# A change to an attention kernel: the weights of rows 4 to 7 are transposed in 32x32 blocks on VectorE and regrouped through DRAM

## The chip, the cores and the metric

The kernel runs on one core of one Trainium2 chip. The metric is the time of one execution on the device in microseconds, the median of repeated runs. The core has TensorE (PE in the profile: matrix products; PEld is its loading of stationary operands), VectorE (DVE), ScalarE (ACT), GpSimd (POOL) and SyncE (SP, which here only issues transfers). They run side by side and wait for one another on semaphores. Operands lie in SBUF (called `arena` here), products are written to PSUM (`psum`, eight banks of 512 float32 columns by 128 partitions). Sixteen DMA engines move data between SBUF and DRAM.

## What is computed

The reference is one inference step of two layers: a gated linear recurrence, and behind it a "forgetting attention" layer over 1024 new positions and, for eight decoding sequences, over 1024 cached positions each. The change concerns the attention over the new positions alone. Cut to that part:

```python
def forgetting_attention(q, k_all, v_all, c_all):
    def one_block(args):                       # 128 query positions
        qi, start = args
        s = jnp.einsum('bqhd,bkhd->bhqk', qi, k_all) * scale
        mask = key_pos[None, :] <= q_pos[:, None]
        logits = jnp.where(mask, s + (c_q[..., :, None] - c_t[..., None, :]), -jnp.inf)
        p = jax.nn.softmax(logits, axis=-1)
        return jnp.einsum('bhqk,bkhd->bqhd', p, v_all)
    out = lax.map(one_block, (qb, starts))
```

There are 16 heads of 64 channels, and everything is float32. The product with the values sums over key positions, so the weights `p`, which come out with query positions on the partitions, must be turned so that key positions lie on the partitions.

## The kernel before

The attention is done in eight pairs of heads (`p` = 0 to 7). Within a pair there are eight rows: row `i` holds the 128 query positions of block `i` against the `i + 1` key blocks up to it, for both heads `x`. Rows are worked as follows, each step on its own engine:

- `scores(p, i)` (L2333, PE) writes the logits to PSUM. Rows 0 to 3 alternate between two halves of banks 2 to 5; rows 4 to 7 fill all four banks, so that such a row can't begin before the one ahead has left them.
- `row_max(p, i)` (L1694 to L1705, DVE) adds the forget bias and the causal mask and takes the maximum.
- `soft(p, i)` (L1175 to L1184, ACT) takes the exponential, sums, and scales the weights; they go to `weights` in SBUF.
- `turn_rows(p, i)` (L2340, PE) transposes them, one 128x128 product with the identity for each head and key block, into the row's banks.
- `turn_a` (L1190, ACT, head 0) and `turn_v` (L1713, DVE, head 1) copy the transposed weights to `pt` in SBUF.
- `weighted(p, m)` (L2356, PE) multiplies rows `2m` and `2m + 1` together with the values, and `fin` (L1724, L1726, DVE) takes the result.

Between these steps, TensorE has other work in hand that fills the time in which a row passes through DVE and ACT: the projections of the next pair, in units of eight products (`kq`, `vg`; L2028, 28 units in a pair, each with an add or copy behind it, L1358 on DVE or L934 on ACT), the means of squares for the norms (L2295), the decoding part (`decode`, L2389), and in the last pair the output projection (`y_part`, L2535). The decoding part streams cached keys and values: SP loads key pages into a ring of two slots (`k_in`, L582, 512 KB each), GpSimd multiplies them with the query (`times_q`, L857), DVE reduces them (`score`, L1767), which frees the slot; value pages come in fours (`v_in`, L588, 4 x 512 KB). SP also loads the projection weights of the pairs ahead (`load_wb`, L471), DVE scales them (`scale_w`, L468), and GpSimd forms sums of them (`block_sums`, L721 to L724) that a unit needs.

The order on every engine is written out by hand in the functions `pair` of the engines; no scheduler changes it. Each engine works its own list in order, and an instruction that waits holds up all that stands behind it on that engine. SP's list of transfers is such a list too.

## Time and profile before

| | |
|---|---|
| median of 3 runs | 1558.84 us (1558.44 to 1559.26) |
| the profiled execution's own time | 1557.86 us |
| its span | 1556.1 us |
| granted TensorE clock, mean over the span | 0.998 |
| TensorE busy | 1525.4 us, 98% |
| VectorE busy | 995.0 us, 64% |
| ScalarE busy | 713.6 us, 46% |
| GpSimd busy | 429.5 us, 28% |
| DMA | 242.32 MB, mean 156 GB/s |

The profile is of one execution; times inside it are counted from the start of its span. The recurrence layer and the first projections take about the first 756 us; the eight pairs follow, about 89 us each, and the rest of the output projection ends the program. Busy time alone doesn't say what a change is worth: the chain of work that ended last and the idle time ahead of each group do that. Matrix products overlap each other, so the mean duration of one in a group is longer than the distance from one to the next; the distance is read from the timeline.

### The profile page before, as it was taken

Reading aid. Unit: us, or ns where it says so; the run is one execution under the profiler, and the core shown is the slowest. Engines: PE = TensorE matmul, PEld = TensorE weight load, DVE = VectorE, ACT = ScalarE, POOL = GpSimd, SP = SyncE. Lnnn points to the kernel's source line nnn. Section 1 sums busy time; section 2 is a strip of 40 time slices with the busy share of each in tenths; the row PEclk is TensorE's granted clock in tenths of the full one; section 3 lists DMA queues with packets and bytes.
Section 4 is the critical chain, followed back from the end, with each engine's and each line's share of the span. In section 5 each row is a group of like instructions: output and inputs, shape, how many; then the busy total and the mean of one; then the engine's idle time right before and its main releaser. Section 6 shows DMA issues by size and latency. Waiting matters only on the chain.

```text
span 1556.1 us, 23869 instructions
## 1 busy us (share of the span) xinstructions
PE 1525.4 (98%) x8769; PEld 1137.0 (73%) x8769; DVE 995.0 (64%) x1947; ACT 713.6 (46%) x1412; POOL 429.5 (28%) x335
## 2 busy tenths in 40 slices
PE   7999999999999999999999999999999999998998
PEld 6888888888888865447777777777777777774443
DVE  6869687876868673226375766667686776765321
ACT  4445554454555542221455655555455564555100
POOL 5022212121231001012253425343343334422200
PEclk9999999999999999999999999999999999999999
DMA  9692936658293743323333445464444546366231
GB/s 270 177 265 78 271 115 199 175 152 242 74 296 102 226 163 99 89 63 100 102 99 111 137 164 176 136 203 136 160 131 134 173 147 193 150 214 231 84 136 56
DMA packets 254085, 242.32 MB, mean 156 GB/s; under 512 B 23162, under 2 KB 219962, under 8 KB 253970
## 3 DMA queue, kind: packets, MB, share of 16 engines
q1 hardware_dynamic: 242834, 204.21, 43.0%
q0 software_dynamic: 11136, 36.59, 6.7%
q8 instruction: 70, 1.15, 0.3%
q14 instruction: 45, 0.37, 0.1%
HBM read 212.63 MB, written 95.24 MB: 198 GB/s over the span
## 4 chain that ended last, share of the span: by engine, by line
PE 90%; DVE 5%; ACT 2%; issue 2%; DMA 0%; SPq 0%; POOL 0%; DVEq 0%; ACTq 0%; POOLq 0%
PE psum L2028 46%; PE psum L2052 7%; PE psum L2535 7%; PE psum L2333 5%; PE psum L2356 4%; PE psum L2340 4%; PE psum L2105 3%; PE psum L2295 2%; PE psum L2389 2%; PE psum L1991 2%; PE psum L2175 1%; PE psum L2116 1%; PE psum L2191 1%; PE psum L2203 1%; ACT arena L1175 1%
## 5 line engine op out<-in xcount | busy, mean ns | idle before, releaser
L2028 PE MATMUL psum<-arena 128*128 128x252 f32 (+1 forms) x3472 | 812.2, 384 | 0.7 <-DVE arena L1358 0.6
L2028 PEld LDWEIGHTS psum<-arena 128*128 128x128 f32 x3472 | 641.6, 190 | 121.1 <-issue 30.5
L1358 DVE TENSOR_TENSOR arena<-arena,psum 128x252 f32<-128x252 f32 (+1 forms) x310 | 130.7, 422 | 216.8 <-PE psum L2028 208.0
L857 POOL TENSOR_TENSOR arena<-arena 128x1024 f32<-128x1024 f32 x64 | 160.4, 2506 | 225.0 <-DMA arena<-k_pages 198.1
L1175 ACT ACTIVATE arena<-psum,arena 128x256 f32<-128x256 f32 (+7 forms) x128 | 93.8, 739 | 122.0 <-DVE arena L1705 121.7
L934 ACT COPY arena<-psum 128x252 f32<-128x252 f32 (+1 forms) x124 | 45.9, 371 | 169.4 <-PE psum L2028 169.4
L2535 PE MATMUL psum<-arena 128*128 128x512 f32 x256 | 114.2, 597 | 0.0
L2052 PE MATMUL psum<-arena 128*128 128x512 f32 x256 | 113.0, 594 | 0.1
L721 POOL TENSOR_TENSOR arena<-arena 128x512 f32<-128x512 f32 x31 | 39.9, 1288 | 249.7 <-issue 129.1
L1184 ACT ACTIVATE arena<-arena 128x256 f32<-128x256 f32 (+7 forms) x128 | 92.4, 769 | 2.1
L2052 PEld LDWEIGHTS psum<-arena 128*128 128x128 f32 x256 | 47.5, 190 | 57.4 <-issue 56.5
L2535 PEld LDWEIGHTS psum<-arena 128*128 128x128 f32 x256 | 46.9, 190 | 56.0 <-issue 55.5
L987 ACT ACTIVATE arena<-arena 128x1024 f32<-128x1024 f32 x48 | 50.6, 1055 | 78.0 <-DVE arena L1402 77.9
L1713 DVE COPY arena<-psum 128x128 f32<-128x128 f32 (+3 forms) x64 | 48.4, 756 | 53.2 <-PE psum L2340 53.1
L2333 PE MATMUL psum<-arena 64*128 64x512 f32 (+3 forms) x384 | 79.3, 517 | 2.1 <-DVE arena L1713 2.0
L2340 PE MATMUL psum<-arena 128*128 128x128 f32 x576 | 76.4, 276 | 4.6 <-ACT arena L1184 4.6
L2340 PEld LDWEIGHTS psum<-arena 128*128 128x128 f32 x576 | 64.9, 141 | 20.4 <-ACT arena L1184 10.9
L1767 DVE TENSOR_REDUCE arena<-arena 128x16 f32<-128x1024 f32 x64 | 77.6, 1213 | 0.0
L2356 PE MATMUL psum<-arena 128*64 128x256 f32 (+1 forms) x640 | 69.5, 362 | 1.6 <-DVE arena L1815 1.6
L2356 PEld LDWEIGHTS psum<-arena 128*64 128x64 f32 x640 | 43.1, 136 | 30.2 <-issue 10.5
L1705 DVE CUSTOM_DVE_ANT_0 psum<-psum,arena 128x128 f32<-128x128 f32 (+3 forms) x128 | 63.4, 536 | 2.2
L1190 ACT COPY arena<-psum 128x128 f32<-128x128 f32 (+3 forms) x64 | 41.3, 646 | 47.2 <-PE psum L2340 45.5
(262 smaller groups left out, 2136.0 us busy)
## 6 DMA issues: line engine op xcount, KB each, us to landing
k_pages<-in_cache_k SPq DMA_DIRECT2D x64, 512.0 KB, 6.7
v_pages<-in_cache_v SPq DMA_DIRECT2D x64, 512.0 KB, 7.2
arena<-k_pages SPq DMA_DIRECT2D x64, 512.0 KB, 3.6
arena<-v_pages SPq DMA_DIRECT2D x64, 512.0 KB, 5.8
arena<-in_w_in_a SPq DMA_DIRECT2D x32, 512.0 KB, 7.0
arena<-in_x_prompt SPq DMA_DIRECT2D x16, 512.0 KB, 7.4
arena<-in_w_kv SPq DMA_DIRECT2D x16, 512.0 KB, 5.5
arena<-in_w_in_b SPq DMA_DIRECT2D x16, 512.0 KB, 7.1
```

The source lines that it names most:

```text
L857: pool.tensor_tensor(k_ring[:, m % 2], k_ring[:, m % 2], q_all[:, m % S:m % S + 1, :].broadcast_to([P, PAGES, P]), ALU.mult).then_inc(kq_m ...
L1175: ins = act.activation(weights[:, x, 0:n], rows[:, x, 0:n], ACT.Exp, bias=top[:, at:at + 1], scale=-1.0, accum_out=total[:, at:at + 1])
L1184: act.activation(weights[:, x, 0:n], weights[:, x, 0:n], ACT.Copy, scale=inv[:, at:at + 1]).then_inc(p_set, 1)
L1358: dve.tensor_tensor(out, more, bank[n % 2][:, 0:size(u)], ALU.add).then_inc(of.by_dve, 1)
L1705: dve.tensor_tensor_reduce(out=rows[:, x, lo:n], in0=rows[:, x, lo:n], in1=c, scale=1.0, scalar=part[:, at:at + 1] if lo else -LOW, op0=AL ...
L1767: dve.tensor_reduce(lg[:, b, :, 0:PAGES].rearrange("p x j -> p j x"), k_ring[:, m % 2].rearrange("p j (x d) -> p j x d", x=2), AX.X, ALU.a ...
L2028: ins = pe.matmul(bank[n % 2][:, 0:size(u)], w[:, k, :], x[:, k, :], start=(k == 0 and r in (0, 1, 3, 4)), stop=(k == HK - 1), skip_group_ ...
L2052: ins = pe.matmul(dst[0:rows, :], o_heads[h][:, rows_of(t)], w_o[:, h, 512 * j:512 * j + 512], start=(h == 0 or lo == AH - 1), stop=(h == ...
L2333: ins = pe.matmul(dst[:, x, lo:hi], q_t[p % 2][rows, cols(i)], k_t[p % 2][rows, lo:hi], start=True, stop=True)
L2340: ins = pe.transpose(row_banks(i)[:, x, cols(j)], weights[:, x, cols(j)], ident)
L2356: ins = pe.matmul(bank[6][rows, lo:2 * P], v_cur[:, j, rows], pt[:, x, SLOT[m] + j, lo:2 * P], start=(j == 0), stop=(j == i), skip_group_c ...
L2535: ins = pe.matmul(dst, o_y[h][:, cols(t)], w_ob[h][:, 512 * j:512 * j + 512], start=(h == 0), stop=(h == AH - 1), skip_group_check=True)
```

## The change

The weights of rows 0 to 3 are still transposed by TensorE, from a smaller buffer (`low_weights`). For rows 4 to 7:

- `soft` leaves the scaled weights in the row's PSUM banks.
- `turn_blocks` (DVE) transposes them out of PSUM into `weights`, once for each head. It transposes within 32x32 blocks only: what is left is to bring each group of 32 partitions' blocks to the partitions of its key positions. `turn_a` and `turn_v` are gone for these rows.
- `store_row` (SP) writes `weights` to a scratch tensor in DRAM, `block_rows`, with four transfers, each from 32 partitions, laid out so that the blocks lie in the wanted order; `load_row` reads the row back into `pt` with one transfer of 128 partitions. A row of block `i` is 2 x (i + 1) x 128 x 128 float32: 0.66, 0.79, 0.92 and 1.05 MB for rows 4 to 7, once out and once in.
- `weighted(p, 2)` and `weighted(p, 3)` wait for the loads (`pt_moved`), and read their moving operand in runs of 32 columns.
- `scores` of rows 5 to 7 and of the next pair's row 0 wait for `blocks_turned`; `turn_blocks` of a row waits until the row ahead is stored (`rows_stored`), since `weights` is one buffer.

Around this the lists of all five engines are ordered anew. `weighted(p, 2)` moves from behind `scores(p, 6)` to behind `scores(p, 7)`; `weighted(p - 1, 3)` moves from just behind `scores(p, 0)` to behind `vg` units 11 and 12; `decode(p - 1, 0)` behind it. The scaling of the four projection weights on DVE, the sums of `w_k` and `w_q` on GpSimd, and the last two key pages of a pair on SP move too.

The core of the diff, part by part; most of the lines that only change places in the lists are left out, since the rows below show them. Layouts and SP's list:

```diff
+        def block_len(i):
+            return 2 * (i + 1) * 32
+
+        def group_len(m):
+            return block_len(2 * m) + block_len(2 * m + 1)
+
+        def moving(m, x, j):
+
+            first, both = 2 * m, j <= 2 * m
+            if m == 0:
+                at, row_step, inner = x * P, 2 * P + x * P, [[1, P]]
+                at, row_step = (at, row_step) if both else (2 * P + x * 2 * P + P, 0)
+            elif m == 1:
+                at, row_step, inner = PT_AT[1] + x * 8 * P + j * 2 * P + (0 if both else P), P, [[1, P]]
+            else:
+                row_step, inner = block_len(first) + 32 * x, [[group_len(m), 4], [1, 32]]
+                at = PT_AT[m] + x * 32 * (first + 1) + 32 * j + (0 if both else row_step)
+            return bass.AP(pt.tensor, pt.offset + at, [pt.ap[0], *([[row_step, 2]] if both else []), *inner])
...
+            def store_row(p, i):
+                sp.wait_ge(blocks_turned, 2 * high_row(p, i))
+                if p:
+                    sp.wait_ge(pt_moved, MOVES * high_row(p - 1, i))
+                n = block_len(i)
+                dst = block_rows[i - LOW_ROWS, :, 0:4 * n].rearrange("(r l) (g n) -> g l r n", r=4, g=4)
+                for g in range(4):
+                    src = weights[32 * g:32 * g + 32, 0:4 * n].rearrange("p (r n) -> p r n", r=4)
+                    sp.dma_start(dst[g], src).then_inc(rows_stored, 16)
+
+            def load_row(p, i):
+
+                m, n = i // 2, block_len(i)
+                sp.wait_ge(rows_stored, STORES * high_row(p, i))
+                if i % 2 == 0:
+                    sp.wait_ge(pv_done, 4 * p + m)
+                at = i % 2 * block_len(i - 1)
+                dst = pt[:, PT_AT[m]:PT_AT[m] + 4 * group_len(m)].rearrange("p (g n) -> p g n", g=4)[:, :, at:at + n]
+                src = block_rows[i - LOW_ROWS, :, 0:4 * n].rearrange("p (g n) -> p g n", g=4)
+                sp.dma_start(dst, src).then_inc(pt_moved, 16)
...
-                    k_in(m - 1)
+                    k_in(m - 2, m - 1)
...
+                k_in(m + 5)
+                store_row(p, 6)
+                load_row(p, 6)
+                store_row(p, 7)
+                load_row(p, 7)
```

GpSimd and ScalarE:

```diff
+                if p + 1 < PAIRS:
+                    sums_of_kq(p + 1)
+                if p:
+                    times_q(m - 2)
...
-                if p + 2 < PAIRS:
-                    sums_of_kq(p + 2)
...
+                dst = low_weights if i < LOW_ROWS else rows
...
-                    ins = act.activation(weights[:, x, 0:n], rows[:, x, 0:n], ACT.Exp, bias=top[:, at:at + 1], scale=-1.0,
+                    if 0 < i < LOW_ROWS:
+                        act.wait_ge(t_done, 2 * low_row(p, i - 1) - 1 + x)
+                    ins = act.activation(dst[:, x, 0:n], rows[:, x, 0:n], ACT.Exp, bias=top[:, at:at + 1], scale=-1.0,
...
-                    act.activation(weights[:, x, 0:n], weights[:, x, 0:n], ACT.Copy, scale=inv[:, at:at + 1]).then_inc(p_set, 1)
+                    act.activation(dst[:, x, 0:n], dst[:, x, 0:n], ACT.Copy, scale=inv[:, at:at + 1]).then_inc(p_set, 1)
...
+                act.wait_ge(t_done, 2 * low_row(p, i) - 1)
+                act.copy(low_pt(i, 0), row_banks(i)[:, 0, 0:(i + 1) * P].rearrange("p (j n) -> p j n", n=P)).then_inc(pt_a, 1)
```

VectorE:

```diff
+            def turn_blocks(p, i, *xs):
+
+                if high_row(p, i) > 1:
+                    dve.wait_ge(rows_stored, STORES * (high_row(p, i) - 1))
+                n = block_len(i)
+                for x in xs:
+                    dve.wait_ge(p_set, 2 * row(p, i) - 1 + x)
+                    out = weights[:, 0:4 * n].rearrange("p (r x j l) -> p x j r l", r=4, x=2, l=32)[:, x]
+                    dve.transpose(out, row_banks(i)[:, x, 0:(i + 1) * P].rearrange("p (j r l) -> p j r l", r=4, l=32)).then_inc(blocks_turned, 1)
...
-                dve.tensor_tensor(g_raw, g_raw, g_tmp, ALU.mult).then_inc(gate_v.sem, 1)
-                dve.wait_ge(gate_v.sem, gate_v.at("silu", p))
-                me.chain(dve.tensor_copy(g_smp[p % 2], g_raw[:, T:N]))
+                me.did(dve.tensor_tensor(g_raw[:, 0:MID], g_raw[:, 0:MID], g_tmp[:, 0:MID], ALU.mult))
+                me.did(dve.tensor_tensor(g_smp[p % 2], g_raw[:, T:N], g_tmp[:, T:N], ALU.mult))
+                dve.tensor_tensor(o_t[:, OWN + p % 2, MID:T], g_raw[:, MID:T], g_tmp[:, MID:T], ALU.mult).then_inc(gate_v.sem, 1)
...
-                turn_v(p, 7)
-                top_of(p, 0)
+                if nxt:
+                    shift(p, 0)
+                turn_blocks(p, 7, 0)
                 if nxt:
                     norm(p + 1, 1)
-                    shift(p, 0)
+                turn_blocks(p, 7, 1)
+                if not nxt:
```

TensorE:

```diff
-                before = TT * p + (i if i >= TT // 2 else max(i - 1, 0))
-                if before:
-                    pe.wait_ge(pt_a, before)
-                    pe.wait_ge(pt_v, before)
+                if 2 <= i <= LOW_ROWS:
+                    last_low = low_row(p, i - 1 if i == LOW_ROWS else i - 2)
+                    pe.wait_ge(pt_a, last_low)
+                    pe.wait_ge(pt_v, last_low)
+                elif i > LOW_ROWS or p:
+                    pe.wait_ge(blocks_turned, 2 * (high_row(p, i - 1) if i > LOW_ROWS else high_row(p - 1, TT - 1)))
...
             def weighted(p, m):
                 i = 2 * m + 1
-                pe.wait_ge(pt_a, row(p, i))
-                pe.wait_ge(pt_v, row(p, i))
+                if i < LOW_ROWS:
+                    pe.wait_ge(pt_a, low_row(p, i))
+                    pe.wait_ge(pt_v, low_row(p, i))
+                else:
+                    pe.wait_ge(pt_moved, MOVES * high_row(p, i))
...
-                        ins = pe.matmul(bank[6][rows, lo:2 * P], v_cur[:, j, rows], pt[:, x, SLOT[m] + j, lo:2 * P],
+                        ins = pe.matmul(bank[6][rows, lo:2 * P], v_cur[:, j, rows], moving(m, x, j),
...
                 if p:
+                    weighted(p - 1, 3)
+                turn_rows(p, 1)
+                if p:
+                    decode(p - 1, 0)
+                vg(p, 13)
+                if p:
                     turn_num(p - 1, 0)
...
-                turn_rows(p, 7)
+                vg_n(5)
+                weighted(p, 2)
```

TensorE's list, from the end of one pair to `weighted(p - 1, 3)` of the next. Before, from `turn_top` (L2366) and the last two units (L2028) of a pair over `scores(p, 0)` (L2333) to `weighted(p - 1, 3)` (L2356):

```order
L2366 MATMUL psum<-arena 8x128 [waits lg_set,items_taken]
L2028 MATMUL psum<-arena 128x264 [waits b_units_taken_v]
L2028 MATMUL psum<-arena 128x264 x3
L2371 MATMUL psum<-arena 128x8 [waits items_taken]
L2028 MATMUL psum<-arena 128x264 [waits b_units_taken_v]
L2028 MATMUL psum<-arena 128x264 x3
L2333 MATMUL psum<-arena 128x128 [waits pt_v,pt_a,norm_done]
L2333 MATMUL psum<-arena 128x128
L2356 MATMUL psum<-arena 64x256 [waits fin_done,pt_v,pt_a]
L2356 MATMUL psum<-arena 64x256 x13
```

After the change, the same place begins later in the pair: `scores(p, 0)`, `vg` 9, the first half of `turn_k`, `vg` 10 and `turn_rows(p, 0)` stand ahead of these rows, which show the second half of `turn_k` (L2379), `scores(p, 1)` (L2413), `turn_smp` (L2385), units 11 and 12 (L2106), and `weighted(p - 1, 3)` (L2439):

```order
L2379 MATMUL psum<-arena 128x128 [waits norm_done,items_taken]
L2379 MATMUL psum<-arena 128x128 x3
L2413 MATMUL psum<-arena 128x256 [waits blocks_turned]
L2413 MATMUL psum<-arena 128x256
L2385 MATMUL psum<-arena 8x128 [waits norm_done,items_taken]
L2386 MATMUL psum<-arena 8x128
L2106 MATMUL psum<-arena 128x264 [waits b_units_taken_a]
L2106 MATMUL psum<-arena 128x264 x3
L2106 MATMUL psum<-arena 128x264 [waits b_units_taken_v]
L2106 MATMUL psum<-arena 128x264 x3
L2439 MATMUL psum<-arena 64x256 [waits fin_done,pt_moved]
L2439 MATMUL psum<-arena 64x256 x13
```

Four projection units, `scores(p, 1)` and the small transposes now stand between `scores(p, 0)` and the product of row 7, and that product waits for the load.

SP's list at the change of pairs. Before, from the loads of `w_k` and `w_q` of one pair to the value pages in the next:

```order
L471 DMA arena<-in_w_kv 128x8x128 [waits b_units_done]
L471 DMA arena<-in_w_in_b 128x8x128
L582 DMA arena<-k_pages 128x1024 [waits k_free] x2
L594 DMA arena<-c_rows 128x1024 [waits max_done]
L591 DMA arena<-c_rows 128x1024 [waits max_done]
L582 DMA arena<-k_pages 128x1024 [waits k_free]
L588 DMA arena<-v_pages 128x1024 [waits num_done]
L588 DMA arena<-v_pages 128x1024 x3
```

After, from the key page `k_in(m + 5)` over the stores and loads of rows 6 and 7 to the value pages (L477 has the two loads ahead of it):

```order
L621 DMA arena<-k_pages 128x1024 [waits k_free]
L667 DMA block_rows<-arena 32x4x448 [waits pt_moved,blocks_turned]
L667 DMA block_rows<-arena 32x4x448 x3
L678 DMA arena<-block_rows 128x4x448 [waits pv_done,rows_stored]
L667 DMA block_rows<-arena 32x4x512 [waits pt_moved,blocks_turned]
L667 DMA block_rows<-arena 32x4x512 x3
L678 DMA arena<-block_rows 128x4x512 [waits rows_stored]
L633 DMA arena<-c_rows 128x1024 [waits max_done]
L630 DMA arena<-c_rows 128x1024 [waits max_done]
L621 DMA arena<-k_pages 128x1024 [waits k_free] x2
L627 DMA arena<-v_pages 128x1024 [waits num_done]
```

The forget biases (`c_rows`) and two key pages now stand behind the load of row 7, which waits for its four stores.

VectorE's list behind row 7's maximum. Before, from the units behind it to the scaling of `w_q` (L468), the last of the pair:

```order
L1358 TENSOR_TENSOR arena<-arena,psum 128x252 [waits b_units_done,b_units_taken_v] x2
L1767 TENSOR_REDUCE arena<-arena 128x8x2 [waits kq_mult]
L1671 SCALAR_TENSOR_TENSOR arena<-arena 128x1032 [waits rs_done]
L1358 TENSOR_TENSOR arena<-arena,psum 128x252 [waits b_units_done,b_units_taken_v]
L1713 COPY arena<-psum 128x8x128 [waits t_done]
L1782 TENSOR_REDUCE arena<-psum 8x1 [waits items_done]
L1671 SCALAR_TENSOR_TENSOR arena<-arena 128x1032 [waits rs_done]
L1788 TENSOR_TENSOR arena<-arena,psum 128x72 [waits items_done]
L1358 TENSOR_TENSOR arena<-arena,psum 128x264 [waits b_units_done,b_units_taken_a]
L1680 TENSOR_TENSOR arena<-arena 64x8 [waits items_done,norm_done]
L1680 TENSOR_TENSOR arena<-arena 64x8
L468 TENSOR_TENSOR arena<-arena 128x1024 [waits w_q_loaded]
```

After, from the unit behind it to the product for the new score (L1748), which is the last of the pair:

```order
L1426 TENSOR_TENSOR arena<-arena,psum 128x252 [waits b_units_done,b_units_taken_v]
L1802 TENSOR_TENSOR arena<-arena,psum 128x256 [waits pv_done]
L1859 TENSOR_REDUCE arena<-psum 8x1 [waits items_done]
L1739 SCALAR_TENSOR_TENSOR arena<-arena 128x1032 [waits rs_done]
L1426 TENSOR_TENSOR arena<-arena,psum 128x252 [waits b_units_done,b_units_taken_v]
L1865 TENSOR_TENSOR arena<-arena,psum 128x72 [waits items_done]
L1790 STREAM_TRANSPOSE arena<-psum 128x8x4x32 [waits p_set,rows_stored]
L1739 SCALAR_TENSOR_TENSOR arena<-arena 128x1032 [waits rs_done]
L1790 STREAM_TRANSPOSE arena<-psum 128x8x4x32 [waits p_set,rows_stored]
L1426 TENSOR_TENSOR arena<-arena,psum 128x264 [waits b_units_done,b_units_taken_a]
L1748 TENSOR_TENSOR arena<-arena 64x8 [waits items_done,norm_done]
L1748 TENSOR_TENSOR arena<-arena 64x8
```

The copy of head 1 (L1713) has become two transposes (L1790), with one of the norms (L1739) between them, and the scaling of `w_q` and one reduction (L1767) have left this place.

## Rows read from the trace of the kernel before

**Rows 1.** Profile page, part 1: busy time of each engine (TensorE is PE).

```profile
PE 1525.4 (98%) x8769; PEld 1137.0 (73%) x8769; DVE 995.0 (64%) x1947; ACT 713.6 (46%) x1412; POOL 429.5 (28%) x335
```

**Rows 2.** Profile page, part 4: the chain that ended last, by engine.

```profile
PE 90%; DVE 5%; ACT 2%; issue 2%; DMA 0%; SPq 0%; POOL 0%; DVEq 0%; ACTq 0%; POOLq 0%
```

**Rows 3.** Windows: length, busy us of each engine, granted clock, DMA share, GB/s.

```profile
1195.87:1285.22 89.35, 88.43 (x598) 67.21 (x597) 64.05 (x137) 49.29 (x105) 36.45 (x24) 1.00 0.49 154
```

**Rows 4.** Timeline, TensorE, places of that pair: start, us, line, tile, count.

```profile
1201.58 0.60 PE L2301 MATMUL psum<-arena 128*128 128x128 f32 x4
...
1238.21 1.35 PE L2340 MATMUL psum<-arena 128*128 128x128 f32 x10
1239.40 0.29 PE L2376 MATMUL psum<-arena 128*128 128x16 f32 x2
...
1263.22 2.61 PE L2356 MATMUL psum<-arena 128*64 128x256 f32 x24
...
1270.92 1.99 PE L2333 MATMUL psum<-arena 64*128 64x512 f32 x8
...
1279.20 1.91 PE L2340 MATMUL psum<-arena 128*128 128x128 f32 x16
1280.95 0.27 PE L2366 MATMUL psum<-arena 128*8 128x128 f32 x1
1281.06 1.95 PE L2028 MATMUL psum<-arena 128*128 128x264 f32 x8
...
1285.22 0.49 PE L2333 MATMUL psum<-arena 64*128 64x128 f32 x4
```

**Rows 5.** Groups by form, TensorE: count, busy us, mean ns of one.

```profile
L2340 PE MATMUL psum<-arena 128*128 128x128 f32 x576 | 76.4, 276 | 4.6 <-ACT arena L1184 4.6
...
L2105 PE MATMUL psum<-arena 128*128 128x128 f32 x448 | 59.9, 277 | 0.0
```

**Rows 6.** Groups by form, VectorE (DVE): copies of L1713, one transpose.

```profile
L1713 DVE COPY arena<-psum 128x1024 f32<-128x1024 f32 x8 | 9.8, 1226 | 6.9 <-PE psum L2340 6.9
...
L1713 DVE COPY arena<-psum 128x640 f32<-128x640 f32 x8 | 6.6, 826 | 3.3 <-PE psum L2340 3.3
...
L1299 DVE STREAM_TRANSPOSE arena<-arena 128x128 f32<-128x128 f32 x1 | 0.3, 311 | 0.0
```

**Rows 7.** Timeline, ScalarE (ACT), the softmax of row 7.

```profile
1274.72 1.12 ACT L1175 ACTIVATE arena<-psum,arena 128x1024 f32<-128x1024 f32 x1 [0.44 <-DVE arena L1705]
...
1277.53 2.19 ACT L1184 ACTIVATE arena<-arena 128x1024 f32<-128x1024 f32 x2
```

**Rows 8.** Timeline, SyncE: four loads issued in a row.

```profile
1250.64 1.93 SPq L588 DMA_DIRECT2D arena<-v_pages  x4
```

**Rows 9.** Line L588, those four loads: time from issue to landing.

```profile
DMA to landing us min/median/max: 3.7/5.3/6.7
```

**Rows 10.** Line L582, 54 loads of 512 KB: time to landing.

```profile
DMA to landing us min/median/max: 3.4/3.6/8.8
```

**Rows 11.** Line L834, eight stores of 512 KB: time to landing.

```profile
DMA to landing us min/median/max: 3.8/8.6/9.0
```

**Rows 12.** Window in which four loads stream: DMA share and GB/s.

```profile
1256.00:1258.00 2.00, 2.00 (x11) 0.99 (x8) 1.43 (x4) 1.06 (x1) 0.00 (x0) 1.00 1.03 395
```

**Rows 13.** Timeline, SyncE, the load of w_v in the same pair.

```profile
1213.72 0.38 SPq L471 DMA_DIRECT2D arena<-in_w_kv  x1
```

**Rows 14.** Timeline, TensorE: one wait and the unit behind it.

```profile
761.06 0.66 PE L2340 MATMUL psum<-arena 128*128 128x128 f32 x2 [1.79 <-ACT arena L1184]
...
762.73 3.04 PE L2028 MATMUL psum<-arena 128*128 128x264 f32 x8
```

**Rows 15.** Windows around that wait, and one in the last pair.

```profile
758.67:761.50 2.83, 1.04 (x7) 0.64 (x5) 0.80 (x5) 2.12 (x9) 0.00 (x0) 1.00 0.00 0
761.50:764.90 3.40, 3.30 (x10) 2.60 (x10) 0.29 (x1) 1.30 (x4) 0.74 (x1) 0.50 0.00 0
1431.00:1437.00 6.00, 4.40 (x24) 2.11 (x22) 5.20 (x18) 3.01 (x7) 1.12 (x1) 1.00 0.06 25
```

178 lines of the change are left out of this document (90 added, 88 removed).

## The prediction

> **What bounds the kernel now.** I read the page's busy times first, then its chain, then windows of one pair, then the timeline inside it. TensorE is busy for 98% of the span [rows 1] and makes 90% of the chain that ended last [rows 2]. In the pair that I take as the pattern, from 1195.87 to 1285.22 us, it is busy for 88.4 of 89.35 us, at a granted clock of 1.00, the 2.4 GHz level [rows 3]. DVE has 25 us to spare in the pair, ACT 40, the DMA engines half their time. So work taken from TensorE's list comes off the time one for one, as long as rows and transfers keep up with the shorter list. That is the whole question.
>
> **What leaves TensorE.** The mean of one transpose is 276 ns [rows 5], but they overlap. The timeline has the distance: the ten of row 4 begin at 1238.21 and the next group at 1239.40, which is 1.19 us; the sixteen of row 7 take 1279.20 to 1280.95, 1.75 us [rows 4]. Rows 5 and 6, with 12 and 14, lie between, so four rows take 4 x (1.19 + 1.75) / 2 = 5.88 us, in eight pairs 47.0 us. Nothing hides them. This is the gain, and no other product leaves: the 416 removed are these.
>
> The Trainium skill ("TensorE: Matmul & The Clock Gate", Part 4: PE-mode transpose) gives a transpose as about 275 ns in one kernel's context. The mean in [rows 5] is the same figure, the distance in [rows 4] is 109 to 119 ns; a sum by the page's figure would take 416 x 0.275 = 114 us off, the sum by the distance 47.
>
> **What the products with the values cost.** Rows 4 to 7 are now read in runs of 32 columns instead of 128. No product here reads such runs. The nearest are those of L2105, whose moving operand is two runs of 64: mean 277 ns against the 276 of the transposes, which read 128 in one [rows 5]. I take 0. If runs half as long doubled nothing at 64, a doubling at 32 is far off; it would cost as much as `weighted` of these rows now takes, about 6 us a pair, and end slower than before. I keep it as a remote end.
>
> **What DVE and ACT get.** Four copies go and eight transposes of the same size come. The one transpose in the trace, 128x128 from SBUF, took 311 ns, a rate like that of the copies (1226 ns for 1024 columns, 826 for 640) [rows 6]. At those, DVE gains 4 x (1.226 + 0.826) / 2 = 4.1 us of work a pair and would stand at 68 of 84 us. ACT loses its four copies. By busy time neither becomes the bound; what counts is when row 7 is ready, since `scores` of the next row 0 waits for it. Before, row 7's scores start at 1270.92 [rows 4], ACT begins the softmax at 1274.72 and finishes scaling at 1279.72 [rows 7], 8.8 us later. In the new order a norm's two steps on ACT come ahead of that softmax and a norm on DVE comes between the two transposes, so I count 8.8 + 0.4 + 1.2 + 1.3 + 1.2 + about 0.5 of queueing = 13.4 us. TensorE's list between the two scores is 1.9 + 0.6 (means) + 4 units of 1.9 + 2.6 (`weighted(p, 2)`, 1263.22) + 0.5 = 13.2 us [rows 4]. So the next pair's row 0 starts with at most a hair's wait. Rows 4, 5 and 6 have chains of 8 to 10 us under 11 to 14 us of list and are covered.
>
> **What the way through DRAM costs.** This is the added wait. Let S be the start of `scores(p, 0)`. On TensorE's list there stand ahead of `weighted(p - 1, 3)`: four units of 1.9, and in small groups two scores (0.4 at 1285.22, and 0.6 for the wider ones), the halves of `turn_k` (0.4 each, 1201.58 without its overlap), row 0's two and `turn_smp`'s two transposes (0.5 together) [rows 4], 9.9 us, with a little between them 10.1 in all; it is wanted at S + 10.1. Row 7 is turned at about S + 0.2. SP issues four transfers in 1.93 us [rows 8]. Four of 512 KB in a row landed after 3.7 to 6.7 us, the last 6.7 us after an issue at the end of those 1.9 [rows 9], so 2.1 MB takes 8.2 us; these four carry 1.05 MB, and the stream of that much less at 340 to 395 GB/s [rows 12] is 3 us shorter: 5.2 us. The load of 1.05 MB is a 512 KB load (median 3.6 us [rows 10]) with 1.5 us more of stream: 5.1 us. Together 10.3 us, ready at S + 10.5: a wait of 0.4 us in quiet. The stores and the load share the engines with key outputs and whatever is late, so it will be more: loads of 512 KB reach 8.8 us [rows 10], stores have a median of 8.6 [rows 11]. Bounds: 0, and with both legs at those longest times 1.9 + 8.6 + 8.8 = 19.3, a wait of 9.4 us. I take 1.5 us, near the quiet end, in 7 pairs (the last pair's product stands behind `y_part`, which covers it): 10.5 us.
>
> Queued behind the waiting product are row 1's transposes, the decoding part and unit 13; DVE's list waits there with `fin(p - 1, 3)`. SP's list is late as well: the forget biases, two key pages, then four value pages, then the key page and the loads of `w_v` and `w_g`. Before, `w_v` was issued 17.9 us after S (1213.72 [rows 13]), when the value pages were long on their way. Now these can start only when `decode` is done, about S + 16, and take 8.2 us; `w_v` lands at about S + 27, and DVE, which wants it ahead of row 3's maximum at S + 25, waits 2 us. Row 3 then reaches TensorE's list about 0.8 us late: 7 x 0.8 = 5.6 us, bounds 0 and 2 x 7 = 14.
>
> **The clock.** A wait can cost twice. In the first pair TensorE waited 1.79 us for row 0 [rows 14], and from 761.50 to 764.90 it was granted half its speed, the 1.2 GHz level [rows 15]; the unit there took 3.04 us in place of 1.95 [rows 4, 14]. In the last pair's stretch with waits of 1.6 us or less the clock stayed at 1.00 [rows 15]. 3.4 us at half speed loses 1.7 us of work. I take it in half of the seven pairs: 6 us, bounds 0 and 12.
>
> **The sum.** -47.0 + 10.5 + 5.6 + 6 = -25 us. The profiled execution took 1557.86 us, 1.0 below the median of the runs; 1557.9 - 25 = 1533, and on the median 1534.
>
> **Rivals.**
> - *The full gain.* All waits near their quiet ends: -47 + 7 x 0.4 = -44, 1515 us. For it: 10.3 against 10.1 us is nearly covered. Against: every other load in flight counts. 0.15.
> - *Half the ports.* Each store takes 32 partitions, and the stream of such a transfer could run at half the rate. The four stores' 1.05 MB then takes 6 us of stream in place of 3: the wait becomes 3.4 us and always brings the clock down. 7 x (3.4 + 1.7) + 5.6 - 47 = -6, 1553 us. No row shows a large transfer from 32 partitions. 0.12. The Trainium skill ("SBUF — State Buffer", Door 1: the DMA port swizzle) says that 32 neighbouring partitions reach only half of the sixteen ports; no row here shows it.
> - *The rows become the chain.* `turn_blocks` of row 6 waits until row 5 is stored, and SP issues those stores behind four value pages and a key page (2.6 MB, 7 us and more of stream at [rows 12]); if the store lands at row 6's softmax end plus 3 us, every later row shifts. 7 x 3 + 10.5 + 5.6 + 6 - 47 = -4, 1555 us, within a hair of no change. For it: DVE is in order and its list is the tightest. Against: 4 us of slack on TensorE's list in row 6. 0.10.
> - *Slower: the way through DRAM lasts 15 us and more.* The wait decides from 7 x (w + 1.7) + 5.6 = 47, that is w = 4.2 us, a way of 14 us against the 10.3 counted. With stores at the median of [rows 11]: 1.9 + 8.6 + 5.1 = 15.6, w = 5.7, and 7 x 7.4 + 5.6 - 47 = +10, 1569 us. For it: those stores are of the same size as half a row. Against: they consist of small pieces, and the value pages, in large ones, landed faster. 0.20.
> - *The mean is the price.* If a transpose took its 275 ns, 114 us would go and 1465 us remain. The distances in [rows 4] speak against it. 0.01.
>
> **How the numbers follow.** My forecast has 0.42, its own range 1522 to 1546. About 0.2% (3 us) is what a measurement of this kernel can tell from no change. Faster: 0.42 + 0.15 + 0.12 + 0.05 of the rows' chain + 0.01 = 0.75; same: 0.05; slower: 0.20. The range of 8 in 10 reaches from a little below the full gain, 1510, to 1562, into the slower case.
>
> **What would show it.** The new profile should have 160 transposes by TensorE in place of 576 and pairs of 84 to 87 us. The wait for the load of row 7 ahead of `weighted(p - 1, 3)` should be 0 to 3 us, seven times; a short 1.2 GHz stretch should follow where it is 1.8 us or more. The time from the first store's issue to the load's landing is the number that decides: near 10 us I am right, near 13 the ports are, above 14 the kernel is slower. A `weighted(p, 2)` of more than the 2.6 us of now, block transposes above 1.3 us for row 7, or gaps ahead of `scores` in rows 5 to 7 would each refute a step. I am wrong altogether if TensorE's idle time in the pairs exceeds 47 us in sum.

## The result and the profile after

The changed kernel took 1576.74 us (median of 4 runs, 1570.37 to 1584.81) beside 1558.64 us for the kernel before on the same chip: ratio 1.012, 95% interval 1.0073 to 1.0167. It is slower by 18 us where 25 us less were forecast, and outside the range. The first fence is the page of the changed kernel (busy times; then the chain that ended last, by engine and by line), answering to [rows 1, 2].

```profile
span 1574.7 us, 23177 instructions
PE 1498.9 (95%) x8353; PEld 1101.0 (70%) x8353; DVE 1008.6 (64%) x1987; ACT 684.7 (43%) x1380; POOL 421.4 (27%) x335
...
PE 74%; DMA 8%; DVE 6%; issue 4%; ACT 4%; POOL 3%; SPq 1%; DVEq 0%; POOLq 0%
PE psum L2106 36%; PE psum L2130 7%; PE psum L2613 7%; DMA arena<-in_w_kv 4%; PE psum L2183 3%; PE psum L2413 3%; DMA block_rows<-arena 2%; PE psum L2439 2%; PE psum L2069 2%; PE psum L2373 1%; DVE arena L474 1%; PE psum L2471 1%; DMA arena<-block_rows 1%; DVE arena L1790 1%; PE psum L2420 1%
```

The 416 transposes are gone, yet TensorE's busy time fell by only 26.5 us (from 1525.4), and its idle time (span less busy time) rose from 30.7 to 75.8 us. Its share of the chain that ended last fell from 90% to 74%, and a weight load, `in_w_kv`, holds 4%, more than both legs of the new way through DRAM.

What TensorE waited for from 750 us to the end (us in total, times, longest):

```profile
PE psum L2420 <- ACT arena L1260: 23.7, 10, 4.2
PE psum L2439 <- DMA arena<-block_rows: 13.0, 7, 2.4
PE psum L2413 <- DVE arena L1790: 9.0, 8, 1.7
```

In order: `turn_rows` for the softmax (rows 0 to 3; 21.0 us of it stand ahead of row 3, in six pairs), the weighted product of row 7 for its load, `scores` for the block transposes. The first is the surprise; for the kernel before the same list reads 4.6 us in 7 times. Its cause stands in the same list for VectorE: `scale_w(w_v)`, waiting for its load.

```profile
DVE arena L474 <- DMA arena<-in_w_kv: 24.7, 6, 4.9
```

Loads of `in_w_kv` from 800 us on, issue to landing, in the changed kernel and then in the kernel before. Every second one is of `w_k`:

```profile
DMA to landing us min/median/max: 6.3/9.2/12.1
```

```profile
DMA to landing us min/median/max: 4.2/5.4/7.8
```

The six of `w_v` alone took 8.7 to 12.1 us, and 4.8 to 5.6 before. The one of the pair shown below, after and before:

```profile
DMA to landing us min/median/max: 11.2/11.2/11.2
```

```profile
DMA to landing us min/median/max: 5.0/5.0/5.0
```

One pair in the timeline (start, duration, engine, line, what, idle time ahead of it). SyncE first: the four stores of row 7, its load, the four value pages, a key page, the load of `w_v`.

```profile
930.14 2.85 SPq L667 DMA_DIRECT2D block_rows<-arena  x4
936.27 0.54 SPq L678 DMA_DIRECT2D arena<-block_rows  x1
...
948.49 1.94 SPq L627 DMA_DIRECT2D arena<-v_pages  x4
951.04 0.32 SPq L621 DMA_DIRECT2D arena<-k_pages  x1
951.41 0.61 SPq L477 DMA_DIRECT2D arena<-in_w_kv  x1
```

VectorE: the copy of row 2, the scaling that waits, row 3's maximum, the scaling of `w_g`; the last line is GpSimd's, a product with a key page.

```profile
957.67 0.55 DVE L1780 COPY arena<-psum 128x384 f32<-128x384 f32 x1
962.65 1.75 DVE L474 TENSOR_TENSOR arena<-arena 128x1024 f32<-128x1024 f32 x1 [4.43 <-DMA arena<-in_w_kv]
964.32 0.42 DVE L1769 TENSOR_TENSOR psum<-psum,arena 128x256 f32<-128x256 f32 x1
...
966.57 2.46 DVE L474 TENSOR_TENSOR arena<-arena 128x1024 f32<-128x1024 f32 x1
...
965.61 2.34 POOL L934 TENSOR_TENSOR arena<-arena 128x1024 f32<-128x1024 f32 x1 [0.88 <-DMA arena<-k_pages]
```

TensorE: row 7's weighted product, row 3's transposes, the unit behind them.

```profile
942.11 1.10 PE L2439 MATMUL psum<-arena 128*64 128x256 f32 x8 [1.89 <-DMA arena<-block_rows]
...
968.30 1.96 PE L2420 MATMUL psum<-arena 128*128 128x128 f32 x8 [3.97 <-ACT arena L1260]
970.05 2.28 PE L2106 MATMUL psum<-arena 128*128 128x252 f32 x6
```

With S = 930.26, `w_v` is issued at S + 21.2 and VectorE starts on it at S + 32.4. Two MB of value pages, issued 3 us earlier, share the DMA engines with it, and these are full from 950 to 962 us (DMA share 1.02, second row below). In the pair of [rows 13] the value pages were issued 9.5 us ahead of `w_v`. Row 3's eight transposes then come 4 us late and take 1.96 us, at half the clock (at full clock 1.04, in e1_scale_back). Windows (TensorE's busy us, the others', granted clock, DMA share, GB/s) of this pair, answering to [rows 3], of the stretch in which `w_v` is awaited, and of the one behind row 3's wait:

```profile
930.26:1022.74 92.48, 84.98 (x546) 63.09 (x546) 63.05 (x143) 45.65 (x101) 35.12 (x24) 0.98 0.69 222
...
950.00:962.00 12.00, 11.86 (x62) 8.50 (x62) 6.19 (x18) 5.09 (x15) 4.32 (x4) 1.00 1.02 326
...
968.30:971.70 3.40, 3.40 (x12) 3.08 (x13) 3.11 (x5) 2.46 (x4) 0.00 (x0) 0.51 0.00 0
```

The pair takes 92.5 us; the six of its kind took 90.2 to 94.4 us, where before they took 88.3 to 89.35 and 84 to 87 were forecast. Stretches at half the clock (mean 0.51 here, the 1.2 GHz level) come seven times from 750 us on, the last 2 us of the program not counted; before it was once. Five follow row 3's waits of 3.7 to 4.2 us, one the way's longest wait (2.4 us), one a wait of `y_part` (2.3 us).

### The profile page after: what moved, and what is told of

The parts are those of the page before. It is cut to its first block, busy times and chain, and to the rows that moved or that the text cites. A ratio compares the mean times of both kernels' runs of the same rounds, so it can differ in the third digit from the quotient of the medians.

```text
span 1574.7 us, 23177 instructions
## 1 busy us (share of the span) xinstructions
PE 1498.9 (95%) x8353; PEld 1101.0 (70%) x8353; DVE 1008.6 (64%) x1987; ACT 684.7 (43%) x1380; POOL 421.4 (27%) x335
## 4 chain that ended last, share of the span: by engine, by line
PE 74%; DMA 8%; DVE 6%; issue 4%; ACT 4%; POOL 3%; SPq 1%; DVEq 0%; POOLq 0%
PE psum L2106 36%; PE psum L2130 7%; PE psum L2613 7%; DMA arena<-in_w_kv 4%; PE psum L2183 3%; PE psum L2413 3%; DMA block_rows<-arena 2%; PE psum L2439 2%; PE psum L2069 2%; PE psum L2373 1%; DVE arena L474 1%; PE psum L2471 1%; DMA arena<-block_rows 1%; DVE arena L1790 1%; PE psum L2420 1%
## 5 line engine op out<-in xcount | busy, mean ns | idle before, releaser
L2106 PE MATMUL psum<-arena 128*128 128x252 f32 (+1 forms) x3472 | 816.2, 386 | 0.9 <-DVE arena L1426 0.9
L2106 PEld LDWEIGHTS psum<-arena 128*128 128x128 f32 x3472 | 645.0, 191 | 121.5 <-issue 26.0
L934 POOL TENSOR_TENSOR arena<-arena 128x1024 f32<-128x1024 f32 x64 | 152.9, 2390 | 369.0 <-DMA arena<-k_pages 364.4
L2613 PEld LDWEIGHTS psum<-arena 128*128 128x128 f32 x256 | 47.7, 192 | 64.1 <-issue 57.0
L1251 ACT ACTIVATE arena<-psum,arena 128x128 f32<-128x128 f32 (+3 forms) x64 | 33.2, 523 | 134.7 <-DVE arena L1773 134.7
L2413 PE MATMUL psum<-arena 64*128 64x512 f32 (+3 forms) x384 | 79.6, 518 | 9.2 <-DVE arena L1790 9.0
L2130 PEld LDWEIGHTS psum<-arena 128*128 128x128 f32 x256 | 47.5, 190 | 57.4 <-issue 56.5
L1251 ACT ACTIVATE psum<-psum,arena 128x640 f32<-128x640 f32 (+3 forms) x64 | 59.0, 921 | 62.2 <-DVE arena L1773 62.2
L2439 PE MATMUL psum<-arena 128*64 128x256 f32 (+1 forms) x640 | 72.0, 370 | 13.0 <-DMA arena<-block_rows 13.0
L2439 PEld LDWEIGHTS psum<-arena 128*64 128x64 f32 x640 | 43.4, 137 | 45.8 <-DMA arena<-block_rows 15.9
L1790 DVE STREAM_TRANSPOSE arena<-psum 128x640 f32<-128x640 f32 (+3 forms) x64 | 63.8, 1027 | 5.2 <-ACT psum L1260 2.7
L474 DVE TENSOR_TENSOR arena<-arena 128x1024 f32<-128x1024 f32 x32 | 50.8, 1609 | 24.8 <-DMA arena<-in_w_kv 24.7
L1762 DVE CUSTOM_DVE_ANT_0 psum<-psum,arena 128x512 f32<-128x512 f32 x64 | 43.1, 716 | 36.3 <-PE psum L2413 36.3
L2413 PEld LDWEIGHTS psum<-arena 64*128 64x128 f32 x384 | 32.2, 187 | 47.3 <-issue 43.2
```

The lines of the kernel that those rows point to most:

```text
L474: dve.tensor_tensor(w, w, gain.unsqueeze(2).broadcast_to([P, KT, P]), ALU.mult).then_inc(scaled, 1)
L934: pool.tensor_tensor(k_ring[:, m % 2], k_ring[:, m % 2], q_all[:, m % S:m % S + 1, :].broadcast_to([P, PAGES, P]), ALU.mult).then_inc(kq_m ...
L1251: ins = act.activation(dst[:, x, 0:n], rows[:, x, 0:n], ACT.Exp, bias=top[:, at:at + 1], scale=-1.0, accum_out=total[:, at:at + 1])
L1790: dve.transpose(out, row_banks(i)[:, x, 0:(i + 1) * P].rearrange("p (j r l) -> p j r l", r=4, l=32)).then_inc(blocks_turned, 1)
L2106: ins = pe.matmul(bank[n % 2][:, 0:size(u)], w[:, k, :], x[:, k, :], start=(k == 0 and r in (0, 1, 3, 4)), stop=(k == HK - 1), skip_group_ ...
L2130: ins = pe.matmul(dst[0:rows, :], o_heads[h][:, rows_of(t)], w_o[:, h, 512 * j:512 * j + 512], start=(h == 0 or lo == AH - 1), stop=(h == ...
```

## The experiments

Kernels are compared with the kernel before on the same chip (medians 1558.2 to 1559.6 us). Names ahead of each edit say on which kernel it rests.

**e1_scale_back: VectorE's order undone.** On the changed kernel:

```diff
-                scale_w(dve, w_v, ...)      # ahead of row_max(p, 3)
-                scale_w(dve, w_g, ...)      # ahead of kq(4)
+                scale_w(dve, w_v, ...)      # behind kq(5)
+                scale_w(dve, w_g, ...)      # behind kq(8)
```

> The changed kernel with one part undone: VectorE's two multiplications by the gain, scale_w(w_v) and scale_w(w_g), go back to where they stood before, behind kq(5) and kq(8), so row_max(p, 3) no longer stands behind a wait for the load of w_v. Theory (the w_v load lands 27 to 32 us after the pair's start, DVE stands before row 3 for it, TensorE then waits 4 us at turn_rows(p, 3) and the clock drops): the 23.7 us that TensorE waited for the softmax in ten places shrink to under 6 us, the half-clock stretches go from nine to four or fewer, and the time is 1538 to 1550 us, below before's 1558.6. Rival 1 (the way through DRAM and its 32-partition stores are the loss, 13 us at the weighted products, and what queues behind them): the time stays above 1565 us. Rival 2 (the DMA queues as a whole are too full, and the next wait is for the same late loads): the wait moves to DVE's scale_w further on, and time is 1560 to 1577 us.

Measured: 1560.0 us, ratio 1.001 (1.0 to 1.0019). The waits of this kernel:

```profile
PE psum L2439 <- DMA arena<-block_rows: 13.3, 7, 2.2
PE psum L2477 <- DVE arena L1879: 12.0, 6, 2.2
PE psum L2413 <- DVE arena L1790: 3.7, 9, 0.9
...
PE psum L2420 <- ACT arena L1260: 2.5, 3, 1.4
```

Row 3's wait went as forecast, but 16.7 us came back and not 27 to 39, and there are still six half-clock stretches. `turn_num` now waits for `smp_sum` on VectorE. `row_max(p, 5)`, the step behind the scaling of `w_g`, did not start later for it: it begins 1.18 us behind its scores in this kernel and in the changed one. What took longer are two of VectorE's products ahead of `smp_sum`, in this kernel (with GpSimd's product beside them) and then in the changed one:

```profile
979.44 1.23 DVE L1812 TENSOR_TENSOR arena<-arena 128x8 f32<-128x8 f32 x1
981.53 2.50 DVE L1820 TENSOR_TENSOR arena<-arena 128x512 f32<-128x512 f32 x1
...
980.60 2.88 POOL L934 TENSOR_TENSOR arena<-arena 128x1024 f32<-128x1024 f32 x1
```

```profile
988.10 0.16 DVE L1812 TENSOR_TENSOR arena<-arena 128x8 f32<-128x8 f32 x1
989.12 0.68 DVE L1820 TENSOR_TENSOR arena<-arena 128x512 f32<-128x512 f32 x1
```

In seven pairs each the long ones began while a product of GpSimd ran, and the short ones beside none. GpSimd's sums of `w_v` and `w_g` wait for the scaling of `w_g`; here they start straight behind it and run into this place. So the later scaling very likely acts through GpSimd. No experiment moved GpSimd's work alone.

**e2_w_first, e3_both: the loads of w_v and w_g first.** SyncE's order on the changed kernel, and on e1_scale_back:

```diff
-                    v_in(p - 1, 1); k_in(m)
                 sp.wait_ge(b_units.done, vg_b(p, 14))
                 load_wb(... w_v ...); load_wb(... w_g ...)
+                    v_in(p - 1, 1); k_in(m)
```

> The changed kernel with SyncE's order alone altered: the loads of w_v and w_g are issued ahead of the four v_pages loads (2 MB) and of one k_pages load, instead of behind them. VectorE's order is the changed one. Theory (w_v is late because it shares the DMA engines with v_pages issued 3 us before it): w_v and w_in_b land in 4 to 6 us instead of 9 to 12, DVE's wait at scale_w falls from 24.7 us in sum to under 8, and the time is 1540 to 1552 us. Rival (w_v is late because its issue waits for TensorE's unit 13 of the pair): its landing is shorter, but the issue stands where it was, DVE still waits 2 us or more in each pair and the time is 1560 to 1572 us.

> Both edits together: scale_w(w_v) and scale_w(w_g) back behind kq(5) and kq(8), and their loads issued ahead of v_pages. Theory: with the scaling back in its place the landing is covered anyway, so this is within 3 us of the first of these kernels (1538 to 1550 us). Rival (the lateness of v_pages and k_pages is what costs, by TensorE's decode or GpSimd's product): this is over 4 us slower than the kernel with the scaling put back alone.

Measured: 1569.09 us (ratio 1.0069, 1.0043 to 1.0095) and 1585.48 us (1.0169, 1.0152 to 1.0186). The theory's time was missed in both. That of e2_w_first lies in its rival's range, but not for the rival's reason: VectorE no longer waits for `w_v`, which lands in 3.9 to 6.0 us. For e3_both its rival holds, 25 us above e1_scale_back. The waits of `turn_rows` fell to 3.6 us in e2_w_first, so the load's landing is their cause; but `k_in(m)` had been moved too. VectorE waits for GpSimd's product with a key page in 13 places, where it did in 6:

```profile
DVE arena L1844 <- POOL arena L934: 25.6, 13, 3.5
```

`score(m)` stands ahead of `turn_v(p, 3)`, for which `scores(p, 4)` waits: 16.9 us in seven pairs. The edit gave one lateness for another. e3_both has this wait (15.1 us) and e1_scale_back's at `turn_num` (11.2 us), and ten half-clock stretches.

**e7_v_last: value pages alone behind the weights.** On the changed kernel, VectorE's order untouched:

```diff
-                    v_in(p - 1, 1)
                     k_in(m)
                 sp.wait_ge(b_units.done, vg_b(p, 14))
                 load_wb(... w_v ...); load_wb(... w_g ...)
+                    v_in(p - 1, 1)
```

> The changed kernel with VectorE's order as changed, and SyncE's order altered so that the four v_pages loads go behind w_v and w_g, while k_pages m keeps its early place ahead of them. (In e2_w_first k_pages m was moved back as well, and VectorE stood before score(m) for it, ahead of turn_v(p, 3), so that scores(p, 4) came 2 to 4 us late in seven pairs.) If v_pages was what made w_v late: w_v lands in under 7 us, the 23.7 us at turn_rows of row 3 fall under 6, scores wait under 3 us for the copies, and the time is 1550 to 1560 us. If row 3 is late for VectorE's two scalings ahead of it whatever they wait for: over 10 us of that wait stay and the time is 1564 us or more.

Measured: 1546.7 us, ratio 0.992 (0.9904 to 0.9937), faster than both kernels, 30 us less than the changed one. The waits, and VectorE in the pair that starts at 924.52:

```profile
PE psum L2439 <- DMA arena<-block_rows: 11.1, 6, 2.1
PE psum L2413 <- DVE arena L1790: 9.4, 8, 2.4
PE psum L2420 <- ACT arena L1260: 3.5, 5, 1.4
```

```profile
952.51 0.55 DVE L1780 COPY arena<-psum 128x384 f32<-128x384 f32 x1
952.98 1.22 DVE L474 TENSOR_TENSOR arena<-arena 128x1024 f32<-128x1024 f32 x1
954.24 0.43 DVE L1769 TENSOR_TENSOR psum<-psum,arena 128x256 f32<-128x256 f32 x1
```

`w_v`, issued at 946.03 (S + 21.5, as before the edit), is there when VectorE comes to it; it lands in 5.5 to 8.6 us in the six pairs. The issue stood where it was; what changed is with whom it shared the DMA engines. Half-clock stretches are four instead of seven. The time is 3 us below the range expected, and `scores` kept its wait of 9.4 us, for which under 3 were expected.

**e4_before_early and e13_before_v_last: the same two edits on the kernel before.**

```diff
 # e4_before_early                       # e13_before_v_last
+ scale_w(dve, w_v, ...)                 - v_in(p - 1, 1)   ahead of k_in(m)
  row_max(p, 3)                          + v_in(p - 1, 1)   behind the load of w_g
```

> The kernel before with one part of the change alone: scale_w(w_v) moved from behind kq(5) to ahead of row_max(p, 3). There is no way through DRAM, no other transfer moved. If the place of the scaling is enough to lose the time, row 3 waits for w_v here too: 2 to 4 us in each of seven pairs and a drop of the clock each time, 1572 to 1590 us. If it takes the fuller DMA queues of the changed kernel (its k_pages load moved behind the pair's end, the block rows), w_v lands in time here and the time is within 5 us of 1558.6.

> The kernel before, with SyncE's order alone altered as in e7_v_last: the four v_pages loads go behind w_v and w_g. If the gain of e7_v_last is the repair of what the change did (w_v late ahead of row 3), there is nothing to repair here, where scale_w(w_v) stands behind kq(5): within 3 us of 1558.6. If the order of these loads is worth something by itself, 1550 us or less, and part of e7_v_last's 30 us is not the change's loss coming back.

Measured: 1565.05 us (1.0038, 1.0025 to 1.0051) and 1563.73 us (1.0029, 1.0014 to 1.0044). In e4_before_early VectorE never waits for `in_w_kv`; the wait of `turn_rows` grows from 4.6 to 9.3 us (10 times, longest 1.8), as row 3 comes 1.2 us later by the scaling's own work. So the place alone costs 7 us, more than the 5 allowed for it and far less than the 13 and more of the other expectation; the late load is missing here. That row 3 is late by the scaling itself is read from the order of the list; no run shows the rest of the 7 us. And the reordering of the loads is no gain by itself: without the change it loses 4 us, a little over the 3 allowed. The 30 us of e7_v_last are the change's own loss and the gain under it.

**e6_no_way: the way through DRAM priced.** On e1_scale_back, `store_row` and `load_row` left out, `weighted` waiting on `blocks_turned`.

> On e1_scale_back, the way through DRAM is left out: no stores, no load, SyncE waits for no block; TensorE's products of rows 4 to 7 wait for VectorE's block transposes alone and read whatever stands in pt, so this leaves out the regrouping. It prices the way with all that hangs on it. If it costs only its wait at row 7: 13.3 us plus the clock drops behind it, 1538 to 1546 us, and w_v and k_pages land as late as before. If its 64 MB of traffic slow the other loads, these land sooner (k_pages 7.2 towards 3.6 us median) and the gain goes beyond 22 us, below 1538. If neither, it stays within 4 us of 1560.

Measured: 1537.45 us, ratio 0.9858 (0.9842 to 0.9875), 22.6 us below e1_scale_back; k_pages land after 4.2 us instead of 7.2. The way costs its 13.3 us of waiting and some 9 behind it: TensorE is busy for 6.8 us less, with three half-clock stretches instead of six, and the rest is other idle time.

This run also settles whether the block rows' traffic is what makes `w_v` late. It is not: with no store and no load of rows, `w_v` still lands in 10.3 to 12.3 us. Value pages and `w_v` in one pair, and the landing of that `w_v`:

```profile
940.03 2.69 SPq L627 DMA_DIRECT2D arena<-v_pages  x4
943.63 0.54 SPq L477 DMA_DIRECT2D arena<-in_w_kv  x1
```

```profile
DMA to landing us min/median/max: 10.3/10.3/10.3
```

The value pages wait for `decode`, which the change moved behind `weighted(p - 1, 3)`. That brings them to 3.6 us ahead of `w_v` in this kernel too.

**e5_ports, e14_spaced_32, e15_spaced_128, e10_ports, e11_all, e12_stores: the shape of the stores.** All keep four stores a row and their bytes. e5_ports, e14_spaced_32 and e15_spaced_128 leave out the regrouping; in the last two the DRAM rows have four pieces 640 columns apart, for the stores and for the load.

```diff
-  for g in range(4):   # changed kernel: 32 partitions, four pieces each
-      dma_start(dst[g], weights[32*g:32*g+32, 0:4*n] as (p, r, n))
+  dma_start(block_rows[i, :, g*n:(g+1)*n], weights[:, g*n:(g+1)*n])   # e5, on e1
+  dma_start(block_rows[i, rows_g, :, 0:n], weights[rows_g] as (p, r, n))  # e14, on e7
+  dma_start(block_rows[i, :, g, 0:n], weights[:, g*n:(g+1)*n])        # e15, on e7
+  dma_start(dst_r as (g 4, l 32, n), weights[:, r*n:(r+1)*n])         # e10 on e7, e11 on e9, e12 on the changed kernel
```

> On the kernel with the scaling put back (e1_scale_back), the four stores of a row take 128 partitions and a quarter of the columns each, instead of 32 partitions and all columns. Bytes, transfers and piece sizes (1.3 to 2 KB) stay. The blocks then land in another order in DRAM, so this leaves out the regrouping, and the weighted sums of rows 4 to 7 are of other numbers. If 32-partition stores reach only part of the DMA engines and this makes the way long, stores and load together shorten by 2 to 4 us per row, the wait at the weighted product of row 7 (13.3 us in seven pairs) falls under 3, and the time is 1540 to 1550 us. If the stores are limited by their issue (0.7 us each) and by other transfers under way, the wait stays within 3 us of 13.3 and the time within 4 us of 1560.

> A clean pair with the next on e7_v_last. Each DRAM row of block_rows has four pieces of n columns, 640 columns apart. Here each of four stores takes 32 partitions and all four pieces. The blocks land in another order, so this leaves out the regrouping. It should be as e7_v_last: row 7's way from store to product 12 us, wait at the weighted product 8 to 13 us in sum, 1543 to 1550 us.

> As the one before, the same bytes to the same addresses in the same pieces, but each of the four stores takes 128 partitions and one piece of each; it too leaves out the regrouping. (In e10_ports the destination's outer dimension was 4 long, and the DMA share fell to 0.3 while those stores ran, so it told of the spreading over engines and not of ports.) If the number of source partitions decides: store of row 7 lands 1 to 1.5 us sooner than in e14_spaced_32, the wait at the weighted product falls under 5 us and the time is 4 to 10 us less. If e5_ports gained by its contiguous destination: same waits and times within 3 us.

Measured: e5_ports 1554.12 us (0.998, 0.9961 to 0.9999), its wait at the weighted product 3.7 us, a gain of 5.9 us on e1_scale_back between its two expectations; e14_spaced_32 1563.6 us (1.0033, 1.0019 to 1.0048), wait 25.1; e15_spaced_128 1537.59 us (0.9873, 0.9847 to 0.9898), wait 4.9. The last two differ in nothing but how the same bytes are divided among stores. Both expectations of a time were missed: e14_spaced_32, with stores from 32 partitions like e7_v_last's, was to be as that kernel and is 17 us slower (in seven pairs its row 7 takes 12.1 to 14.3 us from the first store's issue to the load's landing, e7_v_last's 11.6 to 12.2), which nothing here explains. So the 26 us between the pair are not what the other stores would bring e7_v_last; e15_spaced_128 is 9 us below it. Row 7's stores and load (x, KB each, median us to landing), then SyncE's issue of both, e14_spaced_32:

```profile
block_rows<-arena SPq DMA_DIRECT2D x32, 256.0 KB, 4.3
arena<-block_rows SPq DMA_DIRECT2D x8, 1024.0 KB, 7.4
```

```profile
1018.42 3.27 SPq L667 DMA_DIRECT2D block_rows<-arena  x4
1024.96 0.56 SPq L678 DMA_DIRECT2D arena<-block_rows  x1
```

and e15_spaced_128:

```profile
block_rows<-arena SPq DMA_DIRECT2D x32, 256.0 KB, 2.6
arena<-block_rows SPq DMA_DIRECT2D x8, 1024.0 KB, 5.5
```

```profile
919.60 1.79 SPq L665 DMA_DIRECT2D block_rows<-arena  x4
925.26 0.53 SPq L676 DMA_DIRECT2D arena<-block_rows  x1
```

A store from 32 partitions lands 1.7 us later, and its issue takes SyncE 0.82 us instead of 0.45. So the division costs time; how much is the ports and how much the issue these runs don't part. Nor do they say why the load, the same in both, lands 1.9 us later in e14_spaced_32. The Trainium skill ("SBUF — State Buffer", Door 1: the DMA port swizzle) has 32 neighbouring partitions reach half the ports; the landing agrees in direction, 2.6 against 4.3 us.

> e7_v_last with the four stores of a row cut in another way, into the same DRAM bytes: each takes all 128 partitions and a quarter of the columns (one of the four 32-row groups of the destination), where each took 32 partitions and all columns. The result in DRAM is the same. In e5_ports such stores took 2.8 instead of 4.2 us for row 7 and the wait at the weighted product fell from 13.3 to 3.7 us. If the partitions decide: row 7's store is under 3.2 us here too, the 11.1 us fall under 4 and the time is 1535 to 1542 us. If it was the contiguous destination in DRAM: the store still takes about 4 us and the time is within 3 us of 1546.7.

> Both of the above on e7_v_last. With the wait gone by either edit the other adds little: within 3 us of the better of the two, 1528 to 1540 us. TensorE's idle time from 750 us on is then under 25 us; what is left of it stands at scores for VectorE's block transposes (9.4 us) and at the end.

> The changed kernel itself with the 128-partition stores alone; w_v is late as before. If the ports were the loss, most of the 18 us come back: 1562 us or less. If the loss is w_v's late load, only the wait at the weighted product (13.0 us in seven pairs) shrinks by about 10 us while row 3's 23.7 us stay: 1565 to 1573 us.

Measured: 1710.32 us (1.0969, 1.0951 to 1.0988), 1718.95 us (1.1026, 1.1003 to 1.105) and 1740.26 us (1.1167, 1.1148 to 1.1185): all expectations missed by 160 us and more. A window of e10_ports while, of SyncE's transfers, only row 5's stores run:

```profile
921.00:923.00 2.00, 1.93 (x9) 1.34 (x8) 0.00 (x0) 1.46 (x3) 1.88 (x1) 1.00 0.27 101
```

DMA share 0.27 and 101 GB/s, by estimate about four of sixteen engines: this destination's outer dimension is 4 long, in the others 32 or 128. SyncE issues row 5's stores from 913.27 to 920.05 and can issue the load only at 929.99. The Trainium skill ("DMA: Bandwidth & Descriptors", Why a DMA increments its semaphore by 16 and not by 1) says that the number of engines is the largest up to 16 that divides the slowest dimension of both sides; by this rule it is 4 here, and the trace agrees.

**e8_order, e9_row1, e16_order: where the way is waited for.** TensorE's list around row 1; VectorE's follows it, and in e9_row1 and e16_order ScalarE's copy of row 1 waits for `pv_done`, the products of the pair ahead.

```diff
 # e8_order, on e1_scale_back             # e9_row1, on e7_v_last
- vg(11, 12); weighted(p-1, 3)            + vg(11, 12); turn_rows(p, 1); vg(13)
- turn_rows(p, 1); decode(p-1, 0); vg(13) + weighted(p-1, 3); scores(p, 2)
+ vg(11, 12, 13); weighted(p-1, 3)        + decode(p-1, 0); kq(0); turn_num(p-1, 0)
+ turn_rows(p, 1); decode(p-1, 0)         # e16_order: e9_row1, and scale_w(w_v)
+ turn_num(p-1, 0) behind kq(0)           #   behind row_max(p, 3)
+ turn_num(p-1, 1) behind kq(13)
```

> e1_scale_back with TensorE's list altered where it still waits, and VectorE's with it: weighted(p-1, 3) goes behind unit 13 of the pair (2 us later, so that row 7's load has landed), turn_num(p-1, 0) behind kq(0), and turn_num(p-1, 1) behind kq(13). If these two waits (13.3 and 12.0 us) and the drops of the clock behind them are what keeps e1_scale_back from the gain of the removed transposes: the pair takes 84 to 86 us instead of 88.1 to 89.5 and the time is 1526 to 1540 us. If VectorE is the bound by now (64 of 88 us busy, in a chain with ScalarE), the waits only move on to scores or turn_rows, and the time stays above 1550 us.

> e7_v_last with TensorE's and VectorE's lists altered around row 1: the softmax of row 1 is ready 0.7 us before TensorE reaches the weighted product of row 7 and stands there for the load (1.6 to 2.1 us in six pairs, 11.1 in sum). turn_rows(p, 1) and unit 13 of the pair go ahead of weighted(p-1, 3), scores(p, 2) ahead of decode(p-1, 0), and VectorE's fin, turn_v, row_max(p, 2) ahead of smp_sum and score(m-2). If the way through DRAM is only a matter of where it is waited for: that wait falls under 2 us, row 2's softmax is not late, and the time is 1530 to 1540 us. If, as in e8_order, row 2's softmax becomes late (it waited 1 to 4.6 us in seven pairs there), the time is 1546 us or more.

> e9_row1 with scale_w(w_v) behind row_max(p, 3) instead of ahead of it. In e9_row1 the wait for the way was gone, but turn_rows of row 3 waited 1.3 to 2.4 us in seven pairs for a softmax that comes behind this scaling (1.2 to 1.6 us busy on VectorE). If the scaling ahead of row 3 is by now the last of the change's losses: these waits (13 us) go, a pair takes 84 to 86 us, and the time is 1530 to 1540 us. If the chain of row 3 is late by more than the scaling, or the next row takes its place, the time stays within 4 us of 1548.

Measured: e8_order 1560.0 us (1.0012, 1.0001 to 1.0023), no gain: the two waits fell from 25.3 to 1.6 us and 15.9 us at `turn_rows` came, with 12.5 us at `scores` (3.7 in e1_scale_back), as its second theory had it. e9_row1 1548.5 us (0.994, 0.9922 to 0.9957): the way was no longer waited for, but `turn_rows` waited 17.9 us, 11.5 of it for row 3 behind the scaling. e16_order 1540.5 us (0.9881, 0.9861 to 0.99), the best of those that leave nothing out, 19 us below the kernel before and 36 below the changed one, half a microsecond above the range expected for it. Row 3's waits behind the scaling are gone but for 0.4 to 1.3 us in three pairs, so the scaling's place was worth 8 us here. The shortest of its six pairs, which take 85.6 to 86.5 us:

```profile
923.40:1009.01 85.61, 83.37 (x545) 61.68 (x546) 63.37 (x143) 45.95 (x101) 34.92 (x24) 1.00 0.73 240
```

## Why the prediction was wrong

**The step that failed is "`w_v` lands at about S + 27 ... Row 3 then reaches TensorE's list about 0.8 us late: 7 x 0.8 = 5.6 us, bounds 0 and 2 x 7 = 14".** VectorE got `w_v` at S + 32.4 and row 3 was 3.97 us late. In the six pairs that have this scaling behind a value load (the prediction took seven) row 3 was waited for 21.0 us, above the upper bound. The prediction had seen the order and the 2 MB of value pages. It let them start at S + 16, and all to `w_v` be there 11 us later; they started at S + 18.2, behind a `decode` that had itself slipped, and it took 14.2 us. VectorE so waited 4.4 us and not 2, and nearly all of it reached row 3, where a good microsecond was to be absorbed. Clearing `w_v`'s way gave 30.0 us (e7_v_last), more than the whole loss. Part of that is GpSimd's: in the changed kernel five of the six late scalings of `w_v` began while its key products ran and took 1.75 to 3.0 us instead of 1.2.

- **What leaves TensorE, -47.0.** Right in kind. At full clock a pair holds 83.30 us of products (mean of six, e16_order) instead of 88.16: -4.86 by 8 is -38.9 by estimate, so the term was 8 too large.
- **Runs of 32 columns, 0.** Right: the 80 products of `weighted` in a pair, 56 of them in such runs, have a mean of 364 ns in e16_order and had 362.
- **VectorE's chain at row 7, "at most a hair's wait".** Too small: the next pair's row 0 waited 0.7 to 1.7 us in six pairs, 9.0 us in all at `scores`, though the transposes took 1.24 us for 1024 columns, as the copies did. Rows 5 to 7 had no such wait, so the rival in which the rows become the chain did not come.
- **The way through DRAM, 10.5.** Nearly right in sum, though its parts were not: 13.0 us waited. The way took 12.0 us and not 10.3 (930.14 to 942.11), of which 6.1 to the load's issue, for 5.2, and 5.8 behind it, for 5.1. This is nearer the 13 that the prediction gave to the rival of half the ports than to its own 10, and in e5_ports, with stores from 128 partitions, it took 9.6 to 11.4. So the shape of the stores cost what that rival said in kind; that it is the ports is not shown, and as it leaves out the wait of row 3, it was no account of the loss.
- **The clock, 6.** Too small, for want of the waits that bring it: six more stretches at 1.2 GHz, one of them 6.8 us long. Busy time fell by 26.5 us where e16_order's, with two stretches, fell by 37.2: some 11 us. They came in other places than forecast. The way's waits of 1.8 to 1.9 us in four pairs were followed by no stretch, against the sign that the prediction gave; row 3's of 3.7 us and more were, each time.
- **The slower rival** (a way of 15 us and more) named the wrong place: the way took at most 12.5 us in the changed kernel.

The sum as measured in the profiled execution: TensorE's busy time -26.5, its idle time +45.1, together +18.6 us of span, where -25 were forecast. Of the 44 us between them, 29 are idle time beyond the 16.1 foreseen (about 15 row 3, 7 `scores`, 2.5 the way), 10 are products that did not get as much shorter, and 5 the clock. The test "wrong altogether if TensorE's idle time in the pairs exceeds 47 us" was met by a hair: 54.4 us of waits from 750 us on, 48.4 without those of `y_part`.

## What to carry to other kernels

When a change moves a step ahead of something critical, ask of each load it waits for what is issued within a few microseconds in front of it: queue order, not issue time, decided here, and moving four transfers behind two turned +18 us into -12. Move one transfer at a time, as another that travels with it may be wanted by someone else. And a bottleneck engine that sheds 5% of its work has its whole list's slack shortened: each wait must be looked for again.

## What the runs showed of the hardware

- A store whose DRAM side has an outer dimension of 4 kept about a quarter of the DMA engines busy (share 0.27) and cost the kernel 160 us, though it read all 128 partitions.
- The same bytes from 32 partitions instead of 128 landed in 4.3 instead of 2.6 us, and each transfer took SyncE 0.82 instead of 0.45 us to issue.
- The scaling of 1024 columns on VectorE takes 1.2 us, but 2.46 at 966.57, where it began in the middle of a product of GpSimd. In the changed kernel, from 750 us on, the 11 scalings that began over 0.1 us inside such a product took 1.75 to 3.29 us, the other 17 took 1.20 to 1.23. No experiment moved the one without the other.
